# Two transformer-like blocks with product-key experts on one core: a fixed quarter of the experts through dense matrix products, the rest gathered in rows of 16 KB

## The reference

```python
q = (h @ w_query)                      # split in two halves of 128 per head
v1, i1 = top_k(q_half1 @ keys1.T, 16)  # 128 keys
v2, i2 = top_k(q_half2 @ keys2.T, 16)
top, pos = top_k(v1[:, None] + v2[None, :], 16)
e = i1[pos // 16] * 128 + i2[pos % 16] # an expert, 0 to 16383
gate = softmax(top)
act = down[e] @ h                      # a dot product over 2048
x += sum_k gate[k] * gelu(act[k]) * up[e[k]]
```

## Time and profile before

| | |
|---|---|
| median of 3 runs | 4562.6 us (4559.67 to 4565.71) |
| profiled execution, its span | 4559.0 us, 21846 instructions |
| busy: DVE, POOL, PE, ACT | 3389.3, 2108.9, 1629.2, 397.1 us |
| DMA moved | 1286.59 MB, of it 1073.81 MB by the gathers |

### The profile page before, as it was taken

One profiled execution on the slowest core, in us unless ns is written; L12 is line 12 of the kernel. 1 busy time (PEld: TensorE's weight loads), 2 busy tenths in 40 slices (PEclk: granted clock), 3 DMA queues, 4 the chain that ended last, 5 costly groups with the idle time before them and its releaser, 6 DMA issues. The chain is left out here.

```text
span 4559.0 us, 21846 instructions
## 1 busy us (share of the span) xinstructions
PE 1629.2 (36%) x5521; PEld 961.5 (21%) x5521; DVE 3389.3 (74%) x4309; ACT 397.1 (9%) x780; POOL 2108.9 (46%) x1162
## 2 busy tenths in 40 slices
PE   8999978998900000000000099888000000000000
PEld 6444434444800000000000066457000000000000
DVE  3777795301099999999999913411999999999999
ACT  1111114300100000000000013301000000000000
POOL 0000000000076777776777700000777767767767
PEclk9999989999955555555555599799555555555555
DMA  6343422344399999999999953132999999999999
GB/s 201 111 110 112 117 67 85 103 142 144 126 411 397 379 398 400 378 396 394 388 394 400 374 159 132 56 129 76 405 387 394 400 382 394 408 384 390 398 389 377
DMA packets 283029, 1286.59 MB, mean 282 GB/s; under 512 B 46993, under 2 KB 56033, under 8 KB 150881
## 3 DMA queue, kind: packets, MB, share of 16 engines
q0 software_dynamic: 147456, 1073.81, 57.7%
q1 hardware_dynamic: 100400, 200.81, 13.6%
q10 hardware_dynamic: 35120, 11.33, 1.0%
HBM read 1283.77 MB, written 2.10 MB: 282 GB/s over the span
## 5 line engine op out<-in xcount | busy, mean ns | idle before, releaser
L1578 DVE SCALAR_TENSOR_TENSOR xs<-big,sc,xs 128x2048 f32<-128x2048 f32 x512 | 1203.7, 2351 | 51.0 <-DVE sc L1568 2.1
L1560 DVE CUSTOM_DVE_ANT_0 big<-big,hs 128x2048 f32<-128x2048 f32 x512 | 1137.8, 2286 | 34.8 <-remote 10.3
L488 POOL DMA_INDIRECT big<-in_peer_down,sc x256 | 518.2, 2024 | 638.0 <-issue 635.4
L531 PE MATMUL bank<-wring,ht 128*128 128x512 f32 (+1 forms) x1792 | 778.5, 592 | 3.3 <-ACT ht L888 1.7
L488 POOL DMA_INDIRECT big<-in_peer_u,sc x256 | 518.2, 2024 | 405.0 <-DVE sc L1547 320.4
L488 POOL DMA_INDIRECT big<-in_peer_up,sc x256 | 506.0, 1977 | 247.6 <-DVE xs L1578 172.2
L488 POOL DMA_INDIRECT big<-in_peer_v,sc x256 | 506.1, 1977 | 246.6 <-DVE xs L1578 171.1
L772 PE MATMUL bank<-cn,sc 80*128 80x80 f32 x1 | 0.4, 393 | 1381.4 <-DMA sc<-in_rec_out_norm_g 1381.4
L531 PEld LDWEIGHTS bank<-wring,ht 128*128 128x128 f32 x1792 | 339.7, 192 | 402.1 <-issue 395.9
L545 PE MATMUL bank<-ht,wring 128*128 128x256 f32 x1792 | 387.9, 379 | 2.6 <-ACT ht L888 2.6
L545 PEld LDWEIGHTS bank<-ht,wring 128*128 128x128 f32 x1792 | 340.2, 190 | 49.6 <-issue 2.4
(11 more groups left out here) (308 smaller groups left out, 2055.2 us busy)
## 6 DMA issues: line engine op xcount, KB each, us to landing
wring<-in_w_in SPq DMA_DIRECT2D x84, 1024.0 KB, 5.3
wring<-in_w_out SPq DMA_DIRECT2D x32, 1024.0 KB, 5.0
wring<-in_w_attn_o SPq DMA_DIRECT2D x16, 1024.0 KB, 5.1
wring<-in_peer_w_query SPq DMA_DIRECT2D x16, 1024.0 KB, 5.0
wring<-in_peer_w_q SPq DMA_DIRECT2D x16, 1024.0 KB, 5.0
wring<-in_glu_w_a SPq DMA_DIRECT2D x8, 1024.0 KB, 5.0
wring<-in_glu_w_b SPq DMA_DIRECT2D x8, 1024.0 KB, 5.0
big<-in_peer_down,sc POOLq DMA_INDIRECT x256, 9.5
```

The costliest lines, as they stand in the source:

```text
L488: pool.indirect_dma_start(out=gslot[:, slot, :], out_offset=None, in_=table[0], in_offset=bass.IndirectOffsetOnAxis(ap=usub(rST)[:, b * TO ...
L531: mm = pe.matmul(dense_bank[2 * pair + t][:, 0:w_cols], lhs[:, k, t * P:(t + 1) * P], wslot[:, b, kk * w_cols:(kk + 1) * w_cols], start=(k ...
L1560: v.tensor_tensor_reduce(gslot[:, slot, :], gslot[:, slot, :], h[:, t, :], 1.0, 0.0, ALU.mult, ALU.add, sub(rAC)[:, b * TOPK + kk:b * TOPK ...
L1578: v.scalar_tensor_tensor(x[:, t, :], gslot[:, slot, :], wt[:, kk:kk + 1], x[:, t, :], ALU.mult, ALU.add).then_inc(gused[slot], 1)
```

## The change

The experts whose first key number is below 32 (experts 0 to 4095 of 16384, a quarter) are computed for all 256 tokens as two matrix products on TensorE. The other selections are gathered as before, but another way round.

- **Tables.** The host joins the two tables, so that row e holds the down row and the up row: 16 KB (`peer_rows`). The down rows of experts 0 to 4095 are also given transposed (`dense_down_t`).
- **Gathers.** A step is one head of 8 tokens: its 128 partitions are 8 tokens x 16 selections. One gather a step fetches 128 rows of 16 KB; there are 256 steps in a layer. The expert number of a selection below 4096 is raised by 32768, out of the bounds given to the gather, so that its row is left out. `big` is now four slots of 16 KB (`RING = 4`). A gather waits for `up_used`, which TensorE raises when it has used the slot four steps before.
- **Dot products.** DVE does one for each step (`row_dot`, L1806) against `h_rep`, in which each of the 8 tokens stands on 16 partitions. TensorE makes `h_rep` (`spread_tokens`) and ACT copies it (`take_tokens`), four pieces of 512 columns for 8 steps.
- **Additions.** ACT does the gelu of the step, DVE makes a 128 x 32 block of weights (`weight_block`, L1817), and TensorE sums the up halves of the rows with it in four products of 512 columns, each into another strip of 32 partitions of one PSUM bank (`row_sums`, L913). After each 32 steps DVE adds that bank to x in four pieces (`add_row_sums`).
- **Expert numbers.** `choose` is cut into parts. Eight units (tile 0) are chosen one after another before the first gather, the other eight in pieces between the first 64 steps. Numbers and weights are laid out by step through TensorE (`turn`) and copied back (`collect`).
- **Dense quarter.** SP streams 32 transposed down tables of 1 MB (two slots) and 64 pieces of the up rows of 512 KB (four slots, runs of 4 KB). `down_quarter` is four products of 256 columns, 40 of the 128 before step 0 and one in each step 0 to 87. In steps 96 to 127 the gates of the quarter are made from one-hot matrices (DVE `one_hots`, PE `dense_gates`, DVE `take_gates`). `up_part` is two products of 512 columns, 128 of them in steps 130 to 239, about 7 in 6 steps.

The core of the diff:

```diff
-            def gathers(unit0, down, up):
...
-                        pool.wait_ge(gused[slot], (unit0 + b) * GROUNDS + kk // SLOTS + 1)
...
+            def gathers(layer, rows):
+
+                for s in range(STEPS):
+                    t, g, hd = s // P, s // PH % GRP, s % PH
+                    n = layer * STEPS + s
+                    if s % P == 0:
+                        pool.wait_ge(stage_ready, layer * UNITS + (t + 1) * PH)
+                    if n >= RING:
+                        pool.wait_ge(up_used, n - RING + 1)
+                    i = (t * PH + hd) * GRP + g
+                    pool.indirect_dma_start(
+                        out=row[:, s % RING, :], out_offset=None, in_=rows,
+                        in_offset=bass.IndirectOffsetOnAxis(ap=e_idx[:, i:i + 1], axis=0),
+                        bounds_check=NKEY * NKEY - 1, oob_is_err=False).then_inc(row_full[s % RING], 16)
...
+            def row_sums(layer, s):
...
+                pe.wait_ge(block_ready, n + 1)
+                for q in range(4):
+                    mm = pe.matmul(acc_bank[s // SET % 2][32 * q:32 * q + 32, :], w_block[:, n % BLK, :],
+                                   row[:, s % RING, D + q * 512:D + (q + 1) * 512], start=(s % SET == 0),
+                                   stop=(s % SET == SET - 1), skip_group_check=True)
+                mm.then_inc(up_used, 1)
...
+                for s in range(STEPS):
+                    g, hd = s // PH, s % PH
+                    if hd % 2 and g + 1 < 2 * GRP:
+                        spread_tokens(layer * 2 * GRP + g + 1, hd // 2)
+                    if 0 <= s - FIRST_HOT < 2 * GRP:
+                        dense_gates(layer, s - FIRST_HOT)
...
+                    row_sums(layer, s)
+                    for i in range(quarter_at(s), quarter_at(s + 1)):
+                        down_quarter(layer, i)
+                    for i in range(up_part_at(s), up_part_at(s + 1)):
+                        up_part(layer, i)
...
+                st.link(v.tensor_scalar(sub(rIM), sub(rIX), float(DENSE_E), float(SKIP), ALU.is_lt, ALU.mult))
+                st.link(v.tensor_tensor(sub(rIM), sub(rIM), sub(rIX), ALU.add))
...
+            def row_dot(layer, s):
...
+                if s >= RING:
+                    v.wait_ge(gelu_ready, n - RING + 1)
+                if n:
+                    v.wait_ge(dots_done, n)
+                v.wait_ge(row_full[s % RING], 16 * (n // RING + 1))
+                v.tensor_tensor_reduce(dot_out, row[:, s % RING, 0:D], h_rep[:, n // PH % 2, :], 1.0, 0.0, ALU.mult,
+                                       ALU.add, sub(rAC)[:, n % 4:n % 4 + 1]).then_inc(dots_done, 1)
...
+            def weight_block(layer, s):
...
+                v.wait_ge(gelu_ready, n + 1)
+                if n >= BLK:
+                    v.wait_ge(up_used, n - BLK + 1)
+                v.tensor_scalar(w_block[:, n % BLK, :], col_mask[:, g % 4, :], e_gate[:, i:i + 1],
+                                sub(rGE)[:, n % 4:n % 4 + 1], ALU.mult, ALU.mult).then_inc(block_ready, 1)
...
+                for u in range(PH):
+                    choose(base, u)
...
+                for s in range(STEPS):
+                    row_dot(layer, s)
+                    if s:
+                        weight_block(layer, s - 1)
+                    u = PH + s // 8
+                    if u < UNITS:
+                        if s % 8 == 0:
+                            choose_keys(u, 0)
...
+                        elif s % 8 == 6:
+                            decode(base + u, u)
```

More of the change, by code:

```diff
@@ L753, in peer_scores, with down_quarter @@
                     mm.then_inc(sk_done, 1)
+            def down_quarter(layer, i):
+                r, part = divmod(i, 4)
+                bank = dense_bank[r // 2 % 4]
+                if part == 0:
+                    pe.wait_ge(sdn_full[r % 2], 16 * (layer * (DENSE // 2) + r // 2 + 1))
+                    if r % 2 == 0 and r >= 8:
+                        pe.wait_ge(dd_evac, layer * (DENSE // 2) + r // 2 - 3)
+                for k in range(4 * part, 4 * part + 4):
+                    mm = pe.matmul(bank[:, (r % 2) * T:(r % 2 + 1) * T], sdn[:, r % 2, k * P:(k + 1) * P], hT[:, k, :],
+                                   start=(k == 0), stop=(k == KD - 1), skip_group_check=True)
+                if part == 3:
+                    mm.then_inc(sdn_used, 1)
@@ new lines, in up_part @@
+            def up_part(layer, i):
+                m, t = divmod(i, 2)
+                c, r = divmod(m, DENSE)
+                if i == 0:
+                    pe.wait_ge(dd_evac, (layer + 1) * (DENSE // 2))
+                    pe.wait_ge(gate_evac, (layer + 1) * GRP)
+                if r == 0 and c:
+                    pe.wait_ge(du_evac, 8 * layer + 4)
+                if t == 0:
+                    pe.wait_ge(sup_full[m % 4], 16 * (layer * (DENSE // 2) + m // 4 + 1))
+                for j in range(2):
+                    mm = pe.matmul(dense_bank[2 * t + j][:, :], dense_w[:, r, t * P:(t + 1) * P],
+                                   sup[:, m % 4, j * 512:(j + 1) * 512], start=(r == 0), stop=(r == DENSE - 1))
+                if t == 1:
+                    mm.then_inc(sup_used, 1)
@@ new lines, in turn, with turn_selections @@
+            def turn(n):
+                pe.wait_ge(spread_ready, n + 1)
+                pe.matmul(misc_bank[:, 0:GRP], sub(rCA)[:, 0:P], tok_div, start=True, stop=True)
+                pe.matmul(misc_bank[:, GRP:2 * GRP], sub(rCA)[:, P:2 * P], tok_div, start=True,
+                          stop=True).then_inc(turned, 1)
+            def turn_selections(layer, t):
+                pe.wait_ge(stage_ready, (layer + 1) * UNITS)
+                pe.wait_ge(sel_ready, layer * NT + t)
+                for j in range(3):
+                    tr = pe.transpose(misc_bank[:, j * P:(j + 1) * P], tok_sel[:, t, j, :], ident)
+                tr.then_inc(sel_done, 1)
@@ new lines, in dense_gates @@
+            def dense_gates(layer, hb):
+                n = layer * 2 * GRP + hb
+                pe.wait_ge(hot_ready, n + 1)
+                if hb == 0:
+                    pe.wait_ge(sel_ready, (layer + 1) * NT)
+                elif hb % 2 == 0:
+                    pe.wait_ge(gate_evac, n // 2)
+                for j in range(8):
+                    c = (hb % 2 * 8 + j) * DENSE
+                    mm = pe.matmul(misc_bank[:, c:c + DENSE], hot_b[:, j, :], hot_a[:, j, :], start=True, stop=True)
+                mm.then_inc(gate_done, 1)
@@ new lines, in add_row_sums @@
+            def add_row_sums(layer, j):
+                t, j4 = divmod(j, 4)
+                rows = slice(32 * j4, 32 * j4 + 32)
+                v.wait_ge(up_used, layer * STEPS + (j + 1) * SET)
+                for q in range(4):
+                    xc = x[rows, t, q * 512:(q + 1) * 512]
+                    v.tensor_tensor(xc, acc_bank[j % 2][32 * q:32 * q + 32, :], xc, ALU.add).then_inc(acc_used, 1)
+                v.wait_ge(acc_used, 4 * (layer * 2 * 4 + j + 1))
+                v.sem_inc(x_done, 4)
@@ L1600, in peer_units @@
-                last = base + UNITS - 2
-                unit_down(last, 0, NT - 1)
-                choose(last + 1, 1, base)
-                unit_up(last, 0, NT - 1)
-                unit_down(last + 1, 1, NT - 1)
-                unit_up(last + 1, 1, NT - 1)
+                token_spread(layer)
+                v.wait_ge(sk_evac, 8 * layer + 4)
+                for u in range(PH):
+                    choose(base, u)
+                st.clear()
+                v.wait_ge(sk_evac, 8 * (layer + 1))
```

364 lines of the change are left out of this document (267 added, 97 removed).

## The result

The changed kernel takes **5093.9 us** (median of 4 runs, 5085.9 to 5111.3) against 4562.5 for the kernel before: a ratio of 1.1171, 95% interval 1.1158 to 1.1184. It is slower by 531 us where 76 less was forecast, and it lies above the whole range. The profiled execution has a span of 5085.9 us.

What follows compares the result with a forecast made beforehand. DVE was taken to set the pace, DMA close behind. A changed layer sums 110 + 1231 - 5 + 8 = 1344 us against 1382, 76 less in both: span 4483, plus 3.6 gives 4487 us; range 4310 to 4750.

Steps and rivals of the forecast that it cites:

- The slot's loop: Slot reuse from the landing of s + 1 to that of s + 4: 13.7 us, 4.57 us a step.
- Issue, delay and transfer: Gather part of the slot reuse: POOL issue 0.94, fixed delay 2.3, transfer with stream beside it 5.57 us.
- Its worst case: Slot reuse with POOL's issue held 2.1 us by a dot product: 15.8 us, 5.3 a step.
- 2.0 for the strips, 0.87 for four products: TensorE work per step at full clock: 3.2 of 4.8 us with token spreading, fits; 5.8 at half clock does not.
- One-hot steps: The 34 steps around the one-hot matrices, made in steps 96 to 127: 5.05 us each.
- mostly full: TensorE's clock in the expert layers, taken as mostly full from a granted 0.88 in 20 us of the trace.
- Choices: The first 64 steps, carrying eight more choices on DVE: 4.95 us each against 4.7 for a plain step.
- DMA asks for 4.1 to 4.8: Gather transfers in a layer: 4.1 us for an unstreamed step, 4.8 for a streamed one.
- a fullest engine with 6.6 rows: A gather lands when its fullest DMA engine is done; missing rows clump, so 6.6 rows were taken against 5.96 evenly.
- A: Rival: slot reuse binds, slower, with late POOL issues and half clock at times; 5.3 us a step, 4739 us, chance 0.22.
- B: Rival: rows left out of gathers cost what fetched rows cost; 5.5 us a step, 4840 us, chance 0.10.
- C: Rival: four strips run at once, slot reuse short, DMA near its even share; 4347 us, chance 0.26.

Runs made afterwards that it cites:

- e4: Changed kernel with no dense quarter (no streams, dense products or one-hots), all 32768 rows of a layer gathered, loop untouched: 4962.2 us, ratio 1.088.
- e2: Changed kernel with TensorE spreading tokens behind the row sums instead of behind the dense products: 4982.9 us, ratio 1.092.
- e3: Changed kernel with a step's weights made in its own step, not behind the next landing: 4782.1 us, ratio 1.048.
- e13: e11 with gate products behind the row sums of their step and one-hot matrices in odd instead of even steps: 4631.9 us, ratio 1.015.
- e11: e10 with one one-hot matrix in every second step from 96 to 158 and up products from step 162 on: 4814.3 us, ratio 1.056.
- e5: Changed kernel with the new orders of e2 and e3 together: 4734.2 us, ratio 1.038.
- e10: e5 with the weights directly behind their dot product, ahead of the pieces of choices and one-hot matrices: 4758.4 us, ratio 1.045.
- e6: Changed kernel with selections below expert 4096 neither gathered nor computed: 4813.8 us, ratio 1.056.
- e7: e4 with each step's weights made in its own step, still four slots: 4626.0 us, one run, no interval.
- e8: e4 with six slots instead of four: 4645.9 us, ratio 1.019.

## Why the prediction was wrong

**The step that failed** is "The slot's loop": "13.7 us from the landing of s + 1 to that of s + 4: 4.57 us a step". The form was right, the loop of three steps with the wait for the next landing in it, and it does bind. Its sum was too small: by 3.7 us in the turn of e4, where no dense work disturbs it (17.4), by 2.7 in the turn of the changed kernel (16.4), and by 3.1 in both as the mean of the steps 130 to 239 (16.8). Term by term:

- Dot product, weights and hand-over, 2.3 + 0.3: measured 2.6.
- Strips and hand-over to POOL, 2.0 + 0.3: measured 1.9 at full clock and 2.8 at half.
- Issue, delay and transfer, 0.94 + 2.3 + 5.57 = 8.8, taken from a lone gather: measured 12.0 in e4's turn and 11.4 there in the mean; in the changed kernel 9.6 in the turn shown, 11.1 in the mean of the steps 130 to 239. **This is the largest error.** With four slots a gather is issued while the one before it is still being carried. In e4 the one of 2202.32 was itself held on POOL for 2.8 us and landed by 2214.51, and that of 2207.38 then took 4.9 us more, the length of 2 MB at the full rate. A fixed delay and a transfer of its own do not make the time of a queued gather.
- Not in the sum at all: row sums that find TensorE in a dense product (2.7 us in the turn shown, some 0.5 in the mean of the steps 130 to 239), and a gelu that stands behind the token copy and the spreading. e2 puts a price on the second: 111 us.

The prediction let the loop bind only "where the transfer of the fullest engine lies on it", and took 4.7 between 4.6 and 5.3. Its worst case, 5.3, was itself below the 5.97 measured. e3 shows how much hung on it: with a fourth step in the loop, 312 of the 607 us by which the forecast missed are gone.

**TensorE.** "2.0 for the strips, 0.87 for four products": each product was counted as one instruction, but the earlier trace rows counts instructions, and the kernel has two of them for each product. Four products of 256 columns are thus eight of its instructions, 1.99 us at full clock, and two of 512 are 1.98. The strips erred the other way, 1.07 instead of 2.0. The sum of 3.2 us thus came near the 3.6 measured, with its terms wrong. It fits at full clock, as said, but not always in time for the row sums. At half clock the measured terms (1.94, 3.56, and 2.07 in every second step) add up to 6.5, not to 5.8.

**One-hot steps**, forecast at 5.05: measured 6.87 in 34 steps, 62 us a layer. I priced the DVE work alone. TensorE was taken at "mostly full" clock, and in these steps it is granted half and busy for 178.75 of 200 us (the row of 1950 to 2150 above): 3.62 us for the gate products, 1.94 for the row sums and 2.07 for the spreading in every second step are 6.6 of the 6.87. So here TensorE's work by itself comes near the step. What its queue does while it waits for DVE comes on top: e13 shows it in e11's layout, where the gate products stood ahead of the row sums. How the 6.87 divides in the kernel as changed was read in the trace and not taken apart by a run of its own.

**Choices**, forecast at 4.95: measured 6.47. A third of the excess is the token chain (e2: 5.94), the rest the loop and the place of the weights behind the pieces (e5 5.49, e10 4.88). With the orders repaired the forecast of 4.95 is met.

**Bytes and DMA.** The bytes were right (800.57 MB), and so was the DMA share below full as long as the loop binds. Once it does not, a step takes 4.84 us (e5), just above "DMA asks for 4.1 to 4.8". The reason given for that, a fullest engine with 6.6 rows where an even share has 6, is not shown: no view tells the DMA engines apart. What the trace of e5 does show (2150 to 2550) is a mean share of 0.96, so that the engines together have little idle time left, and 16 KB packets of 650 ns in the mean, where 0.62 us was the price.

**The rivals.** A, the loop, was the right one in kind: POOL's issues take 1.41 us in the mean, instead of 0.99, and the clock drops to half in places. But it gave 4739 us, below the 5094 measured, and the sum was too small for the reasons above. B is refuted: the rows left out cost next to nothing (below), and e6 is faster than e4. C is refuted in its time, though its premise holds: the strips do run at the same time. The Trainium skill ("TensorE: Matmul & The Clock Gate", section on packing small matmuls) says that products into different column strips overlap, and the trace agrees: eight instructions of 512 columns end in 1.07 us where four in a row took 1.88. That saved 0.9 us in a loop whose sum was short of three to four.

**The balance.** Even the repaired kernel loses. What stands here was worked out, not tried. A layer has about 115 us before the first dot product and 9.5 behind the last, so it would need 4.93 us a step to match the 1382 of before, and e13 has 5.05; its stages with streams would stay near the 4.8 of e5 and e10, where DMA is nearly full. The dense quarter saves 0.5 MB of each 2 MB gather and streams 0.25 MB back, and what is left of the gain does not pay for 100 us in which no row is gathered. The comparison of e13 with e7 says the same of the dense quarter: both take 5.05 us a step, and e7 has not even e10's order, which was worth 0.6 us a step beside the choices.

## What to carry to other kernels

A ring of few large slots is a loop: write down every engine from the landing of a slot to the landing of its next use, count over how many steps it closes, and price the transfer as one that is queued behind others, from a full stretch of the trace and not from a lone transfer. An instruction that releases a buffer belongs ahead of everything in its queue that could wait; here 0.3 us of weights moved by one place was worth 312 us, and eight gate products behind the sums instead of ahead, with their matrices moved by a step, 182. Before fewer bytes are bought with more steps in the chain, test whether DMA will still be what the chain waits for.

## What the runs showed of the hardware

- **Strips of TensorE overlap in float32**: four products of 32 columns out and 512 in end in 1.07 us at full and 1.94 at half clock.
- **The hand-over from TensorE to POOL** takes 0.8 us behind the end that the profile models for the last product (2204.62 + 1.94 to 2207.38). From DVE to TensorE it is 0.06 us: the weights of 0.30 us start at 2204.26, the row sums at 2204.62.
- **Rows left out are nearly free**: the number of packets is the same, 73728, with and without the quarter, but a row left out has a packet of 4 bytes, 9 ns, in place of 16 KB, 611 ns at the median. The queue's packet time falls from 54.3% of 4965.8 us (e4) to 41.7% of 5085.9, by 575 us, and to 45.0% of 4815.1 in e6, by 530, where 16679 rows at 611 ns over 16 engines would be 637: the rows that stay took longer in the mean (706 ns in e6, 657 in e4).
- **A gather of 16 KB rows** reaches the same full rate as one of 8 KB rows: 428 GB/s at a DMA share of 1.01 (e8), 422 at 1.01 before.
- **A DMA share near 1 is not the full rate**: e4 shows 0.94 with 374 GB/s, e7 1.01 with 425; a 16 KB packet took 657 ns in the mean in e4's stage, 618 in e7's.
- **A busy TensorE at half clock**: in the one-hot steps of e13 PE is busy for 128.8 of 150 us at a granted clock of 0.50, with many products of 32 columns; in the next stage, 174.5 of 200 us with products of 512, it is 0.96.
